# Two-layer block in fp32 on one core: the feed-forward down product in pairs of column chunks, three of eight steps with seven block products

## The chip, the cores and the metric

One core of a Trainium2 chip. The metric is device time in microseconds (us). A whole two-layer block for 256 tokens of width 2048 runs in one launch. TensorE multiplies, ScalarE (ACT) and VectorE (DVE) prepare operands and read results, SyncE (SP) issues the weight stream, GpSimd (POOL) a few other transfers.

## The reference

Everything is fp32. The part that matters here is the feed-forward of the second layer, with D = 2048 and D_FF = 8192:

```python
u = _rmsnorm(h, norm_mlp_g[layer])
a = jnp.einsum('bsd,df->bsf', u, w_up[layer])
a = jnp.square(jax.nn.relu(a))
h = h + jnp.einsum('bsf,fd->bsd', a, w_down[layer])
return _rmsnorm(h, norm_final_g)
```

## The kernel before, in words

**Exact products from three rounded ones.** Every fp32 operand is split into a rounded part (hi, type f32r) and the rest (lo). A product is three matmuls into the same bank: hi x hi, hi x lo, lo x hi. Activations are split once. Weights are split as they arrive.

**The stream.** All weights lie in one array of 359 units of 128 x 2048 fp32 (1 MB). SyncE loads unit u into slot u mod 4 of `raw`. Each unit is two pieces of 1024 columns. For piece n, ScalarE copies it into `w_hi` (L971, `split`), VectorE subtracts to get `w_lo` (L1404), TensorE uses both. The ring has RING = 4 piece slots: piece n+4 goes into the slot of piece n. `w_used` starts at 4 and TensorE raises it by one behind the last matmul of a piece; ScalarE waits for it, then raises `w_rounded`, VectorE waits for that and raises `w_rest`, which TensorE and SyncE wait for.

**The order of an engine's work.** It is written out by hand. `pieces(n, slot)` on ScalarE and VectorE goes through n pieces of the current product; for the j-th of them it splits the piece that lies four ahead and then calls `slot(j)`, other work put there. Each engine runs its own program strictly in order.

**The feed-forward.** w_up and w_down are cut into four slabs of 2048 hidden columns. A slab first makes the hidden activations in eight chunks of 256 columns (`project_up`, L887 and L890, banks of 512 with hidden columns as rows), four pieces each; VectorE squares them, ScalarE and VectorE split them into m_hi and m_lo. Then follow four down chunks of 512 output columns (`project`, L512 to L514), eight pieces each, for two tiles of 128 tokens. Of proj's four banks a chunk fills two, and the next chunk fills the other two while VectorE adds the finished ones, scaled, to `nat` (`add_scaled`, L1940). Four more banks (tbank, bank_a, bank_b) are idle in the feed-forward. Slabs 1 and 2 are one hardware loop on TensorE, ScalarE and VectorE. The last chunk of all is `project_last`: token tile 0 first, then tile 1, with four extra slots for weights.

**A border between chunks.** VectorE's reads of a finished chunk stand behind the last call of `pieces` for that chunk, and so behind the split of the fourth piece of the next one:

```python
dve.wait_ge(w_rounded, piece.at(1))
V.tensor_tensor(lo[:, s, :], raw[...], hi[:, s, :].bitcast(f32), SUB).then_inc(w_rest, 1)
...
pieces(slot=slot)
if not (end and d == 3):
    add_scaled(d)
```

Of the kernel before, what the change touches and what calls it, by code (L numbers as in the profile page):

```python
# [24 lines left out]
N_SLABS = 4  # L25
# [3 lines left out]
RING = 4  # L29
# [6 lines left out]
UNITS = 1 + 4 * (4 + 4 + 8 + 4 + 2 + 8) + 14 + 4 * (4 + 4 + 4) + 4 * 8 + 4 * 4 + 4 * N_SLABS * 8  # L36

# [76 lines left out]
def build(nc, stream, x_in, consts_in, early_in, params_in, pos_in, dft_in, alibi_in, fg_in, wf_in, z_store, ga_store, gb_store,  # L114
# [6 lines left out]
    with ctx:  # L121
# [59 lines left out]
        fg = place("fg", [P, D], f32, 144.25)  # L181

# [63 lines left out]
        inv3_sq = little("inv3_sq", [P, TT])  # L246
        inv4 = little("inv4", [P, TT])
# [9 lines left out]
        bank_b = psum("bank_b")  # L257
        x_banks = tbank + [proj[2], proj[3], bank_a, bank_b] + tbank
# [91 lines left out]
        tile_done = sem("tile_done")  # L350
        out_ready = sem("out_ready")
# [13 lines left out]

        PIECES = 2 * UNITS


        @block.sync
        def _(sp):  # L370
# [12 lines left out]
            whole, rest = divmod(UNITS - RING, RING)  # L383
# [90 lines left out]
        def _(pe):  # L474
# [423 lines left out]
            def hidden_before(j):  # L898
                pe.wait_ge(m_rest, up.at() - UP_CHUNKS + j + 1)

# [21 lines left out]
            def slab(head=None, before=None, end=False):  # L922
# [6 lines left out]
                if end:  # L929
                    project_last()  # L930
                else:
                    project(m_hi, m_lo)

            def up_head(j):
                if j == 1:
                    m_head(2)
                    m_head(3)

            def up_before(j):
                m_before(2 * j + 1)  # L940

            slab(up_head, up_before)
            with loop(pe, N_SLABS - 2, {piece: 64, chunk: UP_CHUNKS + 4, up: UP_CHUNKS}):
                slab()
            slab(end=True)
# [4 lines left out]
        def _(act):  # L950
            piece, done, chunk, tr, seq = Tally(), Tally(), Tally(), Tally(), Tally()
            sums = Tally()
# [8 lines left out]
            def split(n=1):  # L961
                for _ in range(n):
                    if piece.reg is None and piece.n >= PIECES:
                        return
                    u = piece.n // 2
                    if piece.n % 2 == 0:
# [1158 lines left out]
```

## Time and profile before

| | us |
|---|---|
| median of 3 runs (2145.39 to 2145.77) | 2145.61 |
| profiled execution | 2145.35 |
| its span | 2143.4 |
| TensorE busy | 2120.6 |
| VectorE busy | 1213.8 |
| ScalarE busy | 1022.7 |

The page shows TensorE at a granted clock of nine tenths or more in all 40 slices and busy nine tenths or more in all but the first and the last. Times are microseconds unless marked ns; L12 is line 12 of the kernel; a matmul's own duration (0.39 us for 128x512) overlaps that of its neighbours, so the distance from start to start is what it costs.

### The profile page before, as it was taken

To read this page: it belongs to the slowest core of one execution; us is meant where nothing else is said; L and a number is where in the kernel's file an instruction comes from. 1 tells how busy PE (TensorE), PEld (TensorE's weight loads), DVE (VectorE), ACT (ScalarE), POOL (GpSimd) and SP (SyncE) were. 2 spreads that over 40 slices of the span, in tenths; PEclk is the share of its full clock that TensorE was granted. 3 is DMA by queue.
4 is the path that set the end of the run, shared out by engine and by line. 5 is a ranking of instruction groups with operands and counts; after the bars stand their busy time and mean duration, and the time that the engine had idled before them with its cause. 6 is when DMAs were issued, how large, how long until landed. Compare 5 with 4: busy or idle time off the path is not lost.

```text
span 2143.4 us, 26531 instructions
## 1 busy us (share of the span) xinstructions
PE 2120.6 (99%) x10172; PEld 1772.7 (83%) x10172; DVE 1213.8 (57%) x1508; ACT 1022.7 (48%) x1301; POOL 37.8 (2%) x49
## 2 busy tenths in 40 slices
PE   8999999999999999999999999999999999999998
PEld 7888888888888877788888888888888888888886
DVE  5874545545555775556554454466556555655655
ACT  6444454445444674454454453454434434434443
POOL 0000000000000020000000000000000000000000
PEclk9999999999999999999999999999999999999999
DMA  7555555564565544365755542445555555555553
GB/s 268 177 196 190 189 192 193 196 235 177 177 218 194 190 145 157 121 233 196 291 185 187 179 157 96 177 176 199 195 196 188 186 196 192 183 194 196 183 192 117
DMA packets 56548, 402.44 MB, mean 188 GB/s; under 512 B 6240, under 2 KB 6496, under 8 KB 9216
## 3 DMA queue, kind: packets, MB, share of 16 engines
q1 hardware_dynamic: 53648, 380.67, 49.6%
q0 software_dynamic: 2656, 19.81, 2.4%
q8 instruction: 75, 1.23, 0.2%
q10 hardware_dynamic: 144, 0.52, 0.1%
q14 instruction: 25, 0.20, 0.0%
HBM read 392.59 MB, written 8.39 MB: 187 GB/s over the span
## 4 chain that ended last, share of the span: by engine, by line
PE 97%; ACT 1%; issue 1%; DVE 0%; DMA 0%; SPq 0%; POOLq 0%; POOL 0%; DVEq 0%; ACTq 0%
PE proj L512 25%; PE proj L514 24%; PE proj L513 24%; PE proj L887 11%; PE proj L890 6%; PE tbank L488 2%; PE bank_a L689 1%; ACT w_hi L971 1%; PE bank_a L686 0%; DMA nat<-x 0%; PE proj L817 0%; PE bank_b L843 0%; PE bank_a L831 0%; PE bank_a L767 0%; PE bank_b L783 0%
## 5 line engine op out<-in xcount | busy, mean ns | idle before, releaser
L1404 DVE TENSOR_TENSOR w_lo<-raw,w_hi 128x1024 fp32r<-128x1024 f32 x714 | 873.9, 1225 | 871.1 <-ACT w_hi L971 862.0
L971 ACT ACTIVATE w_hi<-raw 128x1024 fp32r<-128x1024 f32 x714 | 756.8, 1060 | 1043.9 <-PE proj L514 846.5
L512 PE MATMUL proj<-w_hi,a_both 128*128 128x512 f32 x1728 | 686.5, 397 | 0.0
L514 PE MATMUL proj<-w_hi,a_both 128*128 128x512 f32 x1728 | 674.1, 390 | 0.0
L513 PE MATMUL proj<-w_lo,a_both 128*128 128x512 f32 x1728 | 672.6, 389 | 0.0
L514 PEld LDWEIGHTS proj<-w_hi,a_both 128*128 128x128 f32 x1728 | 324.4, 188 | 69.2
L512 PEld LDWEIGHTS proj<-w_hi,a_both 128*128 128x128 f32 x1728 | 324.6, 188 | 68.4 <-issue 4.3
L513 PEld LDWEIGHTS proj<-w_lo,a_both 128*128 128x128 f32 x1728 | 324.9, 188 | 65.0
L887 PE MATMUL proj<-a_both,w_hi 128*128 128x512 f32 x1024 | 256.7, 392 | 0.3 <-DVE a_both L1432 0.3
L887 PEld LDWEIGHTS proj<-a_both,w_hi 128*128 128x128 f32 x1024 | 184.3, 189 | 34.1 <-DVE a_both L1432 0.5
L512 PE MATMUL proj<-w_hi,m_hi 128*128 128x512 f32 x480 | 186.8, 389 | 0.0
L513 PE MATMUL proj<-w_lo,m_hi 128*128 128x512 f32 x480 | 186.8, 389 | 0.0
L514 PE MATMUL proj<-w_hi,m_lo 128*128 128x512 f32 x480 | 186.7, 389 | 0.0
L890 PEld LDWEIGHTS proj<-a_both,w_lo 128*128 128x128 f32 x1024 | 139.7, 190 | 10.0
L890 PE MATMUL proj<-a_both,w_lo 128*128 128x256 f32 x1024 | 142.8, 282 | 0.0
L514 PEld LDWEIGHTS proj<-w_hi,m_lo 128*128 128x128 f32 x480 | 90.1, 188 | 18.8
L512 PEld LDWEIGHTS proj<-w_hi,m_hi 128*128 128x128 f32 x480 | 90.1, 188 | 18.5
L513 PEld LDWEIGHTS proj<-w_lo,m_hi 128*128 128x128 f32 x480 | 90.1, 188 | 18.5
L512 PE MATMUL proj<-w_hi,lat_hi 128*128 128x512 f32 x112 | 45.6, 407 | 0.3 <-DVE v_b L1801 0.3
L514 PE MATMUL proj<-w_hi,lat_lo 128*128 128x512 f32 x112 | 43.9, 392 | 0.0
L513 PE MATMUL proj<-w_lo,lat_hi 128*128 128x512 f32 x112 | 43.7, 390 | 0.0
L1432 DVE SCALAR_TENSOR_TENSOR a_both<-tbank,par,a_both 128x256 fp32r<-128x256 f32 x56 | 24.1, 476 | 9.9 <-ACT a_both L1004 9.8
(298 smaller groups left out, 1169.1 us busy)
## 6 DMA issues: line engine op xcount, KB each, us to landing
raw<-stream SPq DMA_DIRECT2D x359, 1024.0 KB, 4.8
nat<-x SPq DMA_DIRECT2D x4, 512.0 KB, 8.3
z_store<-z POOLq DMA_DIRECT2D x1, 2048.0 KB, 8.2
ga_store<-z POOLq DMA_DIRECT2D x1, 2048.0 KB, 12.4
gb_store<-z POOLq DMA_DIRECT2D x4, 512.0 KB, 7.9
yb<-z_store POOLq DMA_DIRECT2D x4, 512.0 KB, 7.9
ga<-ga_store POOLq DMA_DIRECT2D x1, 2048.0 KB, 8.1
gb<-gb_store POOLq DMA_DIRECT2D x1, 2048.0 KB, 14.3
```

The costliest lines, as they stand in the source:

```text
L488: last = nc.tensor.transpose(tbank[tr.n % 2][:, b * P:(b + 1) * P], src(b), ident)
L512: nc.tensor.matmul(banks[t][:, :], ah, wh, start=first, stop=False)
L513: nc.tensor.matmul(banks[t][:, :], ah, wl, start=False, stop=False)
L514: last = nc.tensor.matmul(banks[t][:, :], al, wh, start=False, stop=end)
L689: last = nc.tensor.matmul(bank_a[:, to:to + keys], qr_t[r, h // 2, t * P:(t + 1) * P], kr_t[r, h // 2, 0:keys], start=False, stop=(t == TT ...
L887: nc.tensor.matmul(banks[f], w_hi[:, s, cols], a_both[:, kt, :, :].rearrange("p s t -> p (s t)"), start=(kt == 0), stop=False)
L890: last = nc.tensor.matmul(banks[f][:, 0:TOK], w_lo[:, s, cols], a_hi[:, kt, :], start=False, stop=(kt == KT - 1))
L971: A((w_hi_end if extra else w_hi)[:, piece.n % RING, :], raw[:, u % RING, (piece.n % 2) * PIECE:(piece.n % 2 + 1) * PIECE], ACT.Copy).then ...
L1404: V.tensor_tensor(lo[:, s, :], raw[:, u % RING, (piece.n % 2) * PIECE:(piece.n % 2 + 1) * PIECE], hi[:, s, :].bitcast(f32), SUB).then_inc( ...
L1432: last = V.scalar_tensor_tensor(lo[:, kt + f, :], b[:, f * TOK:(f + 1) * TOK], par_c(g, i + f), hi[:, kt + f, :].bitcast(f32), MUL, SUB)
```

## The change

The four down chunks of a slab become two pairs of column chunks; seven pairs in all, numbered q = 0 to 6, since the last slab keeps its last two chunks in the old form. A pair is eight steps over the hidden dimension (256 rows each), and a step has all four outputs at once: two token tiles by two column blocks of 512. Its unit of weights has four blocks of 512: two of hidden rows by two of columns. Five steps (0, 2, 4, 6, 7) do the plain eight block products of three matmuls. Steps 1, 3 and 5 do Winograd's form of Strassen's 2x2 product: VectorE adds up four combinations of the weight blocks (`sum_weights`) and four of the activation blocks (`sum_hidden`), and seven block products follow. Four of them go to banks of their own (`mixed`), three into the banks of the plain outputs (`whole`), and VectorE puts mixed ones together into the outputs (`add_mixed`). So a pair uses all eight banks; the next pair swaps the two sets of four.

A summed step's unit takes four ring pieces instead of two (1024, 512, 1024 and 1024 columns, the last two from `w_sum`), a pair 22 pieces. Step 7 (`end_step`) takes the four outputs one after another, tile 1 first, and signals each (`part_done`), but frees its two pieces together at its end. `part_read` counts VectorE's reads, five a pair: one in part 2 of `add_mixed`, four in `add_whole`. The slab loops are written out. The core of the diff (left out: declarations, ScalarE's form of the split, which follows the same table of pieces, the host's order of the blocks in a unit, the unchanged split of the piece table, the two chunks at the end, which keep their matmuls):

```diff
+STEPS = 8
+SUM_AT = (1, 3, 5)
+PAIRS = 2 * N_SLABS - 1
+END_ORDER = (2, 3, 0, 1)
...
+        if u in SUM_UNITS:
+            where += [(u, 0, PIECE, False), (u, PIECE, CW, False), (u, 0, PIECE, True), (u, PIECE, PIECE, True)]
+        else:
+            where += [(u, 0, PIECE, False), (u, PIECE, PIECE, False)]
...
+            def product(bank, hi, lo, wh, wl, first=False, end=False):
+                nc.tensor.matmul(bank[:, :], hi, wh, start=first, stop=False)
+                nc.tensor.matmul(bank[:, :], hi, wl, start=False, stop=False)
+                return nc.tensor.matmul(bank[:, :], lo, wh, start=False, stop=end)
...
+            def plain_step(step, whole):
+                for h in range(2):
+                    pe.wait_ge(w_rest, piece.at(1))
+                    for t in range(TT):
+                        tok = slice(t * P, (t + 1) * P)
+                        for n in range(2):
+                            last = product(whole[2 * t + n], m_hi[:, 2 * step + h, tok], m_lo[:, 2 * step + h, tok],
+                                           *weights(0, n), first=(step == 0 and h == 0))
+                    last.then_inc(w_used, 1)
+                    piece.add()
+            def sum_step(step, whole, mixed):
+                i = SUM_AT.index(step)
+                t0, t1 = slice(0, P), slice(P, TOK)
+                a, b = 2 * step, 2 * step + 1
+                first, end = i == 0, i == len(SUM_AT) - 1
+                pe.wait_ge(w_rest, piece.at(1))
+                product(mixed[0], m_hi[:, a, t0], m_lo[:, a, t0], *weights(0, 0), first=first, end=end)
+                product(whole[0], m_hi[:, b, t0], m_lo[:, b, t0], *weights(0, 1)).then_inc(w_used, 1)
+                piece.add()
+                pe.wait_ge(ms_rest, sums.at(i + 1))
+                pe.wait_ge(w_rest, piece.at(1))
+                product(whole[1], ms_hi[:, i, 3, :], ms_lo[:, i, 3, :], *weights(0, 0)).then_inc(w_used, 1)
+                piece.add()
+                pe.wait_ge(w_rest, piece.at(1))
+                product(mixed[1], ms_hi[:, i, 1, :], ms_lo[:, i, 1, :], *weights(0, 0), first=first, end=end)
+                product(mixed[3], ms_hi[:, i, 0, :], ms_lo[:, i, 0, :], *weights(0, 1), first=first,
+                        end=end).then_inc(w_used, 1)
+                piece.add()
+                pe.wait_ge(w_rest, piece.at(1))
+                product(mixed[2], ms_hi[:, i, 2, :], ms_lo[:, i, 2, :], *weights(0, 0), first=first, end=end)
+                product(whole[2], m_hi[:, b, t1], m_lo[:, b, t1], *weights(0, 1)).then_inc(w_used, 1)
+                piece.add()
+            def end_step(step, whole):
+                pe.wait_ge(w_rest, piece.at(2))
+                for o in END_ORDER:
+                    tok = slice(o // 2 * P, (o // 2 + 1) * P)
+                    for h in range(2):
+                        last = product(whole[o], m_hi[:, 2 * step + h, tok], m_lo[:, 2 * step + h, tok],
+                                       *weights(h, o % 2), end=(h == 1))
+                    if o != END_ORDER[-1]:
+                        last.then_inc(part_done, 1)
+                last.then_inc(w_used, 2)
+                piece.add(2)
+            def pair(q):
+                whole, mixed = parts[q % 2], parts[1 - q % 2]
+                if q:
+                    pe.wait_ge(part_read, 5 * (q - 1) + 1)
+                else:
+                    pe.wait_ge(t_by_dve, by_dve.at())
+                for step in range(STEPS):
+                    if q % 2 == 0:
+                        pe.wait_ge(m_rest, up.at() - UP_CHUNKS + step + 1)
+                    if step == SUM_AT[0]:
+                        if q % 2 == 0:
+                            pe.wait_ge(proj_read, chunk.at() * 2)
+                        else:
+                            pe.wait_ge(part_read, 5 * q)
+                    if step in SUM_AT:
+                        sum_step(step, whole, mixed)
+                    elif step == STEPS - 1:
+                        end_step(step, whole)
+                    else:
+                        plain_step(step, whole)
...
+            for n in range(N_SLABS):
                 for c in range(UP_CHUNKS):
                     up.add()
-                    project_up(slot=head if c == 0 else None, before=before if c == 0 else None)
-                project(m_hi, m_lo, before=hidden_before)
-                for j in range(2):
+                    if n and c < 2:
+                        pe.wait_ge(part_read, 5 * (2 * n - 1) + (3, 5)[c])
+                    assert chunk.n % 2 == 1 - c % 2
+                    first = n == 0 and c == 0
+                    project_up(slot=(lambda j: (m_head(2), m_head(3)) if j == 1 else None) if first else None,
+                               before=(lambda j: m_before(2 * j + 1)) if first else None)
+                pair(2 * n)
+                if n < N_SLABS - 1:
+                    pair(2 * n + 1)
+                else:
+                    pe.wait_ge(part_read, 5 * (PAIRS - 1) + 1)
                     project(m_hi, m_lo)
...
+            def round_sums(i):
+                act.wait_ge(ms_summed, ms_sums.at(i + 1))
+                A(ms_hi[:, i, :, :], ms[:, :, :], ACT.Copy).then_inc(ms_rounded, 1)
...
+            def pair(q):
+                for step in range(STEPS):
+                    def slot(j):
+                        if q % 2 == 0 and step == 0 and j == 0:
+                            round_hidden(UP_CHUNKS - 1)
+                        if step == SUM_AT[-1] + 1 and j == 0:
+                            act.wait_ge(w_used, done.at(RING))
+                            if q % 2:
+                                act.wait_ge(part_read, 5 * (q - 1) + 1)
+                            else:
+                                act.wait_ge(proj_read, chunk.at() * 2)
+                            A(stg[:, 0, :], parts[1 - q % 2][0][:, :], ACT.Copy).then_inc(m_copied, 1)
+                    pieces(4 if step in SUM_AT else 2, slot=slot)
...
+                    u, at, width, summed = WHERE[piece.n]
+                    s = piece.n % RING
+                    if u in SUM_UNITS and piece.n == FIRST_PIECE[u]:
+                        sum_weights(u)
+                    src = raw[:, u % RING, at:at + width]
+                    if summed:
+                        src = w_sum[:, (w_sums.n - 1) % 2, at:at + width]
                     dve.wait_ge(w_rounded, piece.at(1))
-                    u, s = piece.n // 2, piece.n % RING
                     extra = piece.reg is None and piece.n >= PIECES - RING
                     hi, lo = (w_hi_end, w_lo_end) if extra else (w_hi, w_lo)
-                    V.tensor_tensor(lo[:, s, :], raw[:, u % RING, (piece.n % 2) * PIECE:(piece.n % 2 + 1) * PIECE],
-                                    hi[:, s, :].bitcast(f32), SUB).then_inc(w_rest, 1)
+                    V.tensor_tensor(lo[:, s, 0:width], src, hi[:, s, 0:width].bitcast(f32), SUB).then_inc(w_rest, 1)
                     piece.add()
+            def sum_weights(u):
+                dve.wait_ge(raw_landed[u % RING], (u // RING + 1) * 16)
+                b = raw[:, u % RING, :].rearrange("p (b c) -> p b c", b=4)
+                s = w_sum[:, w_sums.n % 2, :].rearrange("p (b c) -> p b c", b=4)
+                w_sums.add()
+                wait(dve, w_rest, piece.n - 4)
+                V.tensor_tensor(s[:, 0:2, :], b[:, 0:3:2, :], b[:, 3, :].unsqueeze(1).to_broadcast([P, 2, CW]),
+                                ADD).then_inc(w_summed, 1)
+                dve.wait_ge(w_summed, w_sums.at() * 2 - 1)
+                chain(V.tensor_tensor(s[:, 2, :], s[:, 0, :], b[:, 2, :], ADD))
+                V.tensor_tensor(s[:, 3, :], s[:, 2, :], b[:, 1, :], ADD).then_inc(w_summed, 1)
...
+            def sum_hidden(c):
+                dve.wait_ge(up_squared, up.at(c + 1))
+                wait(dve, ms_rest, ms_sums.at(SUM_AT.index(c)))
+                m = stg2[:, c % 2, :].rearrange("p (b c) -> p b c", b=4)
+                V.tensor_tensor(ms[:, 0, :], m[:, 0, :], m[:, 1, :], ADD)
+                chain(V.tensor_tensor(ms[:, 1, :], m[:, 1, :], m[:, 3, :], SUB))
+                chain(V.tensor_tensor(ms[:, 2, :], m[:, 3, :], ms[:, 0, :], SUB))
+                V.tensor_tensor(ms[:, 3, :], m[:, 2, :], ms[:, 2, :], ADD).then_inc(ms_summed, 1)
+            def rest_of_sums(i):
+                dve.wait_ge(ms_rounded, ms_sums.at(i + 1))
+                V.tensor_tensor(ms_lo[:, i, :, :], ms[:, :, :], ms_hi[:, i, :, :].bitcast(f32), SUB).then_inc(ms_rest, 1)
+            def add_mixed(q, part):
+                mixed, n1 = parts[1 - q % 2], 2 * (q % 2)
+                out = lambda t, n: nat[:, t, (n1 + n) * CW:(n1 + n + 1) * CW]
+                u, w = stg[:, 0, :], stg[:, 1, :]
+                if part == 0:
+                    dve.wait_ge(w_used, done.at(RING))
+                    wait(dve, part_read, 5 * q)
+                    dve.wait_ge(m_copied, q + 1)
+                    V.scalar_tensor_tensor(out(0, 0), u, inv3_sq[:, 0:1], out(0, 0), MUL, ADD).then_inc(dve_seq, 1)
+                    seq.add()
+                    chain(V.tensor_tensor(u, mixed[2][:, :], u, ADD))
+                    chain(V.tensor_tensor(w, mixed[1][:, :], u, ADD))
+                if part == 1:
+                    chain(V.tensor_tensor(u, mixed[3][:, :], u, ADD))
+                    V.scalar_tensor_tensor(out(0, 1), w, inv3_neg[:, 0:1], out(0, 1), MUL, ADD).then_inc(dve_seq, 1)
+                    seq.add()
+                    chain(V.scalar_tensor_tensor(out(1, 0), u, inv3_neg[:, 1:2], out(1, 0), MUL, ADD))
+                if part == 2:
+                    V.tensor_tensor(w, mixed[1][:, :], u, ADD).then_inc(part_read, 1)
+                    dve.wait_ge(part_read, 5 * q + 1)
+                    V.scalar_tensor_tensor(out(1, 1), w, inv3_sq[:, 1:2], out(1, 1), MUL, ADD).then_inc(dve_seq, 1)
+                    seq.add()
+            def add_whole(q):
+                whole, n1 = parts[q % 2], 2 * (q % 2)
+                dve.wait_ge(dve_seq, seq.at())
+                for i, o in enumerate(END_ORDER):
+                    t, n = o // 2, o % 2
+                    if i < 3:
+                        dve.wait_ge(part_done, 3 * q + i + 1)
+                    else:
+                        dve.wait_ge(w_used, done.at(RING))
+                    y = nat[:, t, (n1 + n) * CW:(n1 + n + 1) * CW]
+                    V.scalar_tensor_tensor(y, whole[o][:, :], inv3_sq[:, t:t + 1], y, MUL, ADD).then_inc(part_read, 1)
+            def pair(q):
+                for step in range(STEPS):
+                    def slot(j):
+                        if q % 2 == 0 and step == 0 and j == 1:
+                            rest_of_hidden(UP_CHUNKS - 1)
+                        if step == SUM_AT[-1] + 1:
+                            add_mixed(q, j)
+                        if step == SUM_AT[-1] + 2 and j == 0:
+                            add_mixed(q, 2)
+                    pieces(4 if step in SUM_AT else 2, slot=slot)
+                add_whole(q)
...
```

On ScalarE and VectorE the slab is now: eight up chunks with `sum_hidden`, `round_sums` and `rest_of_sums` in their slots, then `pair(2 * n)` and, but in the last slab, `pair(2 * n + 1)`.

## Rows read from the trace of the kernel before

**Rows 1.** The page: span, and busy us, share and instructions by engine.
```profile
span 2143.4 us, 26531 instructions
PE 2120.6 (99%) x10172; PEld 1772.7 (83%) x10172; DVE 1213.8 (57%) x1508; ACT 1022.7 (48%) x1301; POOL 37.8 (2%) x49
```
**Rows 2.** The page: the chain that ended last, by engine.
```profile
PE 97%; ACT 1%; issue 1%; DVE 0%; DMA 0%; SPq 0%; POOLq 0%; POOL 0%; DVEq 0%; ACTq 0%
```
**Rows 3.** Stretches: an up and a down product (PE, PEld, DVE, ACT, POOL; PEclk, DMA, GB/s).
```profile
1605.56:1694.75 89.19, 89.19 (x512) 78.49 (x512) 53.55 (x55) 40.99 (x46) 0.00 (x0) 1.00 0.54 189
1694.75:1782.00 87.25, 87.23 (x387) 71.93 (x385) 45.68 (x42) 34.96 (x34) 0.00 (x0) 1.00 0.55 193
```
**Rows 4.** Timeline at a chunk's end: start, duration, operation, count, idle before and releaser.
```profile
1779.30 1.06 ACT L971 ACTIVATE w_hi<-raw 128x1024 fp32r<-128x1024 f32 x1 [1.66 <-PE proj L514]
...
1781.37 0.39 PE L513 MATMUL proj<-w_lo,m_hi 128*128 128x512 f32 x1
...
1781.59 0.39 PE L514 MATMUL proj<-w_hi,m_lo 128*128 128x512 f32 x1
...
1782.00 2.10 PE L887 MATMUL proj<-a_both,w_hi 128*128 128x512 f32 x8
1782.02 1.06 ACT L971 ACTIVATE w_hi<-raw 128x1024 fp32r<-128x1024 f32 x1 [1.66 <-PE proj L514]
1783.11 1.23 DVE L1404 TENSOR_TENSOR w_lo<-raw,w_hi 128x1024 fp32r<-128x1024 f32 x1 [1.49 <-ACT w_hi L971]
...
1784.25 1.64 DVE L1940 SCALAR_TENSOR_TENSOR nat<-proj,inv_sq,nat 128x512 f32<-128x512 f32 x2
```
**Rows 5.** Groups of instructions, 1500 to 2143 us: busy, mean ns, idle before.
```profile
L1404 DVE TENSOR_TENSOR w_lo<-raw,w_hi 128x1024 fp32r<-128x1024 f32 x224 | 274.5, 1226 | 266.5 <-ACT w_hi L971 263.7 <-DVE nat L1940 2.1
L971 ACT ACTIVATE w_hi<-raw 128x1024 fp32r<-128x1024 f32 x224 | 237.8, 1061 | 349.7 <-PE proj L514 192.4 <-PE proj L890 157.3
...
L1940 DVE SCALAR_TENSOR_TENSOR nat<-proj,inv_sq,nat 128x512 f32<-128x512 f32 x30 | 22.4, 747 | 2.2 <-DVE nat L1940 0.8
L1932 DVE TENSOR_TENSOR m_lo<-stg,m_hi 128x512 fp32r<-128x512 f32 x27 | 18.5, 684 | 0.0
...
L1338 ACT ACTIVATE m_hi<-stg 128x512 fp32r<-128x512 f32 x27 | 16.5, 612 | 0.0
...
L1977 DVE TENSOR_TENSOR nat<-nat,fg 128x1024 f32<-128x1024 f32 x3 | 3.6, 1216 | 0.0
```
**Rows 6.** Timeline: two VectorE operations, the second waiting for the first.
```profile
1442.55 0.68 DVE L1962 TENSOR_TENSOR stg<-proj,stg 128x512 f32<-128x512 f32 x1
...
1443.27 0.69 DVE L1966 SCALAR_TENSOR_TENSOR stg<-stg 128x512 f32<-128x512 f32 x1
```
**Rows 7.** The page: issues of the weight stream, KB each, us to landing.
```profile
raw<-stream SPq DMA_DIRECT2D x359, 1024.0 KB, 4.8
```
**Rows 8.** Timeline: TensorE released by VectorE after a short wait.
```profile
1435.49 1.65 DVE L1432 SCALAR_TENSOR_TENSOR a_both<-tbank,par,a_both 128x256 fp32r<-128x256 f32 x4
...
1437.20 2.14 PE L887 MATMUL proj<-a_both,w_hi 128*128 128x512 f32 x8 [0.31 <-DVE a_both L1432]
```
**Rows 9.** The end: TensorE's last matmul, then two stretches with the granted clock.
```profile
2134.96 0.39 PE L918 MATMUL proj<-w_hi_end,m_lo 128*128 128x512 f32 x1
...
2136.50:2137.00 0.50, 0.00 (x0) 0.00 (x0) 0.08 (x1) 0.39 (x2) 0.00 (x0) 1.00 0.00 0
2137.00:2137.50 0.50, 0.00 (x0) 0.00 (x0) 0.23 (x2) 0.00 (x0) 0.15 (x1) 0.85 0.00 0
```
**Rows 10.** Timeline of TensorE at the start.
```profile
12.29 1.11 PE L555 MATMUL bank_a<-cst,nat 128*128 128x128 f32 x4 [1.64 <-DMA nat<-x]
...
14.05 1.91 PE L555 MATMUL tbank<-cst,nat 128*128 128x128 f32 x8
...
17.26 0.41 PE L572 MATMUL proj<-a_both,w_hi 128*128 128x256 f32 x1
17.47 0.38 PE L573 MATMUL proj<-a_both,w_lo 128*128 128x256 f32 x1
...
18.63 0.28 PE L573 MATMUL proj<-a_both,w_lo 128*128 128x256 f32 x1
18.75 0.28 PE L571 MATMUL proj<-a_both,w_hi 128*128 128x256 f32 x1
```

More of the change, by code:

```diff
@@ L257, in build @@
         bank_b = psum("bank_b")
+        parts = (tbank + [bank_a, bank_b], proj)
         x_banks = tbank + [proj[2], proj[3], bank_a, bank_b] + tbank
@@ L920, in project_last, with weights @@
                 chunk.add()
-            def slab(head=None, before=None, end=False):
+            def product(bank, hi, lo, wh, wl, first=False, end=False):
+                nc.tensor.matmul(bank[:, :], hi, wh, start=first, stop=False)
+                nc.tensor.matmul(bank[:, :], hi, wl, start=False, stop=False)
+                return nc.tensor.matmul(bank[:, :], lo, wh, start=False, stop=end)
+            def weights(ahead, half, k=0):
+                s = (piece.n + ahead) % RING
+                cols = slice(half * CW, (half + 1) * CW)
+                return w_hi[:, s, cols], w_lo[:, s, cols]
@@ L928, in slab @@
                     project(m_hi, m_lo)
-                if end:
                     project_last()
[L931 to L944, printed above, removed]
@@ L945, in _ @@
-            slab(end=True)
+                sums.add(len(SUM_AT))
             assert piece.n == PIECES, (piece.n, PIECES)
@@ L1356, in slab, with slot @@
                     chunk.add()
-                for d in range(4):
-                    def slot(j, d=d):
-                        if d == 0 and j == 1:
-                            round_hidden(UP_CHUNKS - 1)
-                        if end and d and j == 3:
-                            res_squares(d - 1, 16 + 8 * (N_SLABS - 1) + 2 * d)
-                    pieces(slot=slot)
-                    chunk.add()
-                up.add(UP_CHUNKS)
-            up = Tally()
-            slab(first=True)
-            with loop(act, N_SLABS - 2, {piece: 64, done: 64, chunk: UP_CHUNKS + 4, up: UP_CHUNKS}):
-                slab()
-            slab(end=True)
+                pair(2 * n)
+                if n < N_SLABS - 1:
+                    pair(2 * n + 1)
+                up.add(UP_CHUNKS)
+                ms_sums.add(len(SUM_AT))
+            def slot(j):
+                if j in (3, 5):
+                    act.wait_ge(part_read, 5 * PAIRS)
+                    chunk_squares((j - 3) // 2)
+            pieces(slot=slot)
+            chunk.add()
+            pieces(slot=lambda j: res_squares(2, 18) if j == 3 else None)
+            chunk.add()
             for t in range(TT):
-                act.wait_ge(res_ready, 16 + 8 * N_SLABS - 1 + t)
+                act.wait_ge(res_ready, 19 + t)
                 square_sum(stg2[:, t, :], nat[:, t, 3 * CW:4 * CW], ss2[:, t, 3:4])
@@ L1386, in _ @@
         def _(dve):
-            piece, done, chunk, tr, seq, his = (Tally() for _ in range(6))
+            piece, done, chunk, tr, seq, his, w_sums = (Tally() for _ in range(7))
             V = nc.vector
@@ L1966, in slab @@
                     V.scalar_tensor_tensor(s, s, 0.0, s, MAX, MUL).then_inc(up_squared, 1)
[L1967 to L1988 removed]
+                pair(2 * n)
+                if n < N_SLABS - 1:
+                    pair(2 * n + 1)
+                up.add(UP_CHUNKS)
+                ms_sums.add(len(SUM_AT))
+            pieces(slot=lambda j: weigh((j - 4) // 2) if j in (4, 6) else None)
+            add_scaled(2)
+            pieces(slot=lambda j: weigh(2) if j == 4 else None)
             def last_chunk(t):
@@ L2021, in _units_up, with _pair_units @@
     return v.reshape(-1, P, 4 * CW)
+def _pair_units(w):
+    v = w.reshape(STEPS, 2, P, 2, 2, CW)
+    r = np.empty((2, STEPS, P, 4, CW), w.dtype)
+    for step in range(STEPS):
+        order = ((0, 0), (1, 0), (1, 1), (0, 1)) if step in SUM_AT else ((0, 0), (0, 1), (1, 0), (1, 1))
+        for b, (k, n) in enumerate(order):
+            r[:, step, :, b, :] = v[step, k, :, :, n, :].transpose(1, 0, 2)
+    return r.reshape(-1, P, 4 * CW)
 def _stream(i):
```

111 lines of the change are left out of this document (70 added, 41 removed).

## The prediction

> **What bounds the kernel now.** First the page's busy times: TensorE is busy 99% of the span, VectorE and ScalarE about half [rows 1]. Then the chain that ended last: 97% of it is TensorE [rows 2]. So a matmul saved is its time saved, provided TensorE never waits. Then the stretches of one slab: the up product fills 89.19 of 89.19 us, the down product 87.23 of 87.25 us, with VectorE busy 53.55 and 45.68 us [rows 3]. The timeline of a chunk border gives the beat: consecutive 128x512 matmuls start 0.22 to 0.23 us apart, and ScalarE starts rounding one weight piece 2.72 us after another (1779.30, 1782.02), twelve matmuls, 0.2267 us each [rows 4]. A down step of two pieces (24 matmuls) is 5.44 us. This is the arithmetic to keep for everything below.
>
> The same rows show what the prediction turns on: how far VectorE runs ahead. Both splitting engines stay four pieces ahead, and piece n+4 goes into the slot that piece n frees. Let T be the moment when the next matmul would start if nothing waited (1781.59 + 0.23 = 1781.82). The last piece of the chunk frees its slot, ScalarE starts at T+0.20 (1782.02), VectorE's subtraction at T+1.29 (1783.11), and only then, at T+2.43 (1784.25), comes VectorE's first read of the finished banks, because in VectorE's program it stands behind that subtraction. Today this is free: the next chunk writes the other two of proj's four banks [rows 4].
>
> **What is removed.** Three steps in each of seven pairs need 7 block products of three matmuls instead of 8: 7 x 3 x 3 = 63 matmuls, 63 x 0.2267 = 14.3 us, on the path. Nothing else leaves TensorE. The slab loops are unrolled; a loop's return cost 1782.00 - 1781.82 = 0.2 us [rows 4], which I count as nothing, the more so since unrolled code must be fetched.
>
> **What VectorE gets inside a pair.** Single operations, 128x1024 subtraction 1.226, 128x512 0.684, with a bank as input and a scale 0.747, a broadcast input 1.216 us [rows 5]. An operation that waits for the one before starts 0.72 us after it (1442.55, 1443.27) [rows 6]; one that doesn't starts 1.14 us after a 1.23 us subtraction (1783.11, 1784.25) [rows 4], 0.09 earlier. A summed step: three additions of weights 1.26 + 0.72 + 0.60 = 2.6 (the 1024-wide one first, by the broadcast row; the trace has no addition of this very kind, so its ends are the 0.68 of a 512-wide and twice that), subtractions 1.14 + 0.60 + 1.14 + 1.14 = 4.0, together 6.6 us beside 21 x 0.2267 = 4.76 us of TensorE. A plain step: 2.3 beside 5.44. Mixed outputs 5.6 (eight operations), whole outputs 2.8, late hidden rest 0.6. Sum of a pair: 3 x 6.6 + 5 x 2.3 + 5.6 + 2.8 + 0.6 = 40.3 us beside 3 x 4.76 + 5 x 5.44 = 41.5 us. That is 97% full, so I followed it piece by piece: a step that begins at 0 with piece 0. In the first pair of a slab piece 6 is ready at 9.7 and wanted at 10.2, piece 8 at 14.6 against 15.6, piece 14 at 24.4 against 25.8. The four-piece ring carries each surplus of 1.9 us into the plain step behind it. Inside a pair I count no stall; if each summed step ran 0.5 us over, that would be 21 x 0.5 = 10 us. ScalarE has 3 x 1.06 + 0.6 = 3.8 us in a summed step, under 4.76, and costs nothing [rows 5]. In the up product the sums of activations (four small operations and a 0.68, under 3 us for a chunk of 11.2 us) fit in 89.19 - 53.55 = 35.6 us of free VectorE time [rows 3]. The stream moves the same bytes; a unit lands 4.8 us after its issue and is asked for four units ahead [rows 7], so I leave it at nothing; the weight additions also need it at most one step earlier than the rounding does.
>
> **What the pair's borders get.** Now there are eight outputs in eight banks, and the next product needs banks that VectorE has still to read. The last read of the mixed outputs (add_mixed part 2) stands in step 7 behind the split of piece 24 of the pair (22 pieces, so the third of the next phase). That piece goes into the slot of piece 20, the first of step 7, and end_step frees both its pieces only after its last matmul. So whatever the early signals part_done say, VectorE is stuck on w_rounded, which is stuck on w_used, until T. Parts 0 and 1 are done before: step 6's first piece ends at T-8.16, its successor is rounded by T-6.9, three operations and the next subtraction run to T-2.45, three more to T-0.3.
>
> (a) From the first pair of a slab to the second, three times: VectorE first sums the weights of the next pair's step 1 (T-0.3 to T+2.3), subtracts piece 24 (to T+3.45) and makes the last read (0.72, T+4.2). TensorE restarted 0.06 us after such a release (1435.49 + 1.65 = 1437.14, 1437.20) [rows 8]. Stall 4.2 us, 12.6 in all.
> (b) From pair 6 to the plain chunk 2: no sum of weights, so subtraction from T+1.3, read from T+2.45, stall 3.2 us.
> (c) From a second pair to the next up product, three times: TensorE asks for three reads, the mixed one and two whole ones. Read T+2.45 to 3.17, its scaled add to 3.85, split of the 25th piece to 5.0, two scaled adds with a bank (0.67 and 0.75) to T+6.4. Stall 6.5 us, 19.5 in all.
>
> The second waits (a pair's step 1, the second up chunk) come 5.4 and 11.2 us later, when the four whole outputs are read (T+4.2 to T+9 against T+9.6 in (a)): nothing, with 0.5 us to spare. Stalls together 12.6 + 3.2 + 19.5 = 35.3 us. The bounds: if additions of weights cost half, (a) is 3.2 (-3 us); if VectorE enters the border 1.5 us late, (a) grows by that and (b) and (c) don't (+4.5).
>
> **The clock.** TensorE has no idle gap as long as these in the body of this trace. At the end, its last matmul ends at 2134.96 + 0.39 = 2135.35 and the granted clock, 1.00 until 2137.0, reads 0.85 in the half microsecond behind: it fell to half (1.2 of 2.4 GHz) at about 2137.35, 2.0 us after the last work [rows 9]. Every stall above is longer. At the start, 128x256 matmuls came 0.21 us apart (17.26, 17.47) and 0.12 apart later (18.63, 18.75); the engine had then worked without a gap since 14.05, and nearly since 12.29 [rows 10]. The change of beat falls at 17.68, so a return at half rate lasts 3.6 to 5.4 us and costs half of that, 1.8 to 2.7 us. I take 2.0 us and five of the seven stalls, all three of 6.5 us and two of the others: 10 us. Ends: none, 0; all seven at 2.7, 19 us. The Trainium skill, "TensorE: Matmul & The Clock Gate" (Part 1), has half rate as the default that only sustained activity lifts, and its section "HAM oscillation" charges half of all throttled time. The trace agrees in both halves; no row of it shows a gap in the middle of work.
>
> **Sum.** The profiled execution took 2145.35 us (span 2143.4), 0.26 below the median shown. 2145.35 - 14.3 + 35.3 + 10 = 2176.4; plus 0.26, 2176.6 us. Behind the last matmul nothing changes: chunks 2 and 3 of the last slab keep their form, and the squares and gains of the first two columns move into chunk 2, where each engine is half idle.
>
> **Rivals.**
> 1. The stalls come, the clock holds: 2145.6 - 14.3 + 35.3 = 2166.6. For it: the fall at the end follows a gap that never ended. Against: 2.0 us were enough. The skill's page would side with the forecast for the longest gaps.
> 2. VectorE is late inside the pairs as well. For it: 40.3 of 41.5 us, and a margin of 0.5 us at piece 6. Ten more microseconds at 0.5 us a summed step, and (a) grows by 4.5: 2176.6 + 15 = 2191.
> 3. The other side: VectorE reaches the reads before TensorE needs the banks. It decides whether the split in step 7 waits for that step's end. Were piece 24's slot free at the middle of end_step (T-2.7), the last mixed read would end at T+0.5 to T+1.5 and the first whole reads at T+3.8, and with one piece less in front before T: the 63 matmuls would be the result, 2145.6 - 14.3 = 2131.3. Against: two w_used increments come together on the last matmul, and today's reads come at T+2.43 in every chunk.
> 4. The sums don't shorten the product. 7 products of 3 matmuls in the diff leave no room; a change of the beat could. Without the 14.3 us: 2190.9.
>
> **How the numbers follow.** Forecast 0.60; rival 1 0.17; rival 2 0.12; rival 4 0.03; rival 3 0.04; a half way to it that ends near no change 0.04. The range 2158 to 2192 us goes 8 us under rival 1 (stalls of some 27 instead of 35 us) and up to rival 2; that leaves out 2 in 10. What a measurement of this kernel can tell from no change is about 0.2%, 4.3 us. Faster 0.05, same 0.02, slower 0.93.
>
> **What would show it.** In the profile after: 63 matmuls fewer; idle before seven groups of matmuls, released by VectorE, of 4.2 (three), 3.2 (one) and 6.5 us (three); a granted clock under 1.00 in about five short stretches behind them, with 128x512 matmuls 0.43 us apart; the last mixed read in each pair behind a weight subtraction, 2.4 to 3.5 us after end_step's last matmul; VectorE over 90% busy in the pairs and no TensorE gap inside them. It is wrong if the borders show gaps under 1 us, if the gaps lie inside summed steps, or if matmuls keep their 0.2267 us right behind a 6.5 us gap.

## The result and the profile after

The changed kernel takes 2179.71 us (median of 5 runs, 2178.94 to 2182.61) against 2145.53 us: ratio 1.0161, 95% interval 1.0147 to 1.0175. It is 34.2 us slower with 63 matmuls fewer. The forecast was 2176.6. The five runs differ more than those of the kernel before, and the slowest has the lowest mean granted clock (0.989, the others 0.991 and 0.992).

The page of the kernel after: span, busy times by engine, the chain by engine. They answer to [rows 1, 2].

```profile
span 2176.9 us, 25919 instructions
PE 2119.2 (97%) x10109; PEld 1768.6 (81%) x10109; DVE 1352.8 (62%) x1730; ACT 1064.7 (49%) x1362; POOL 37.8 (2%) x49
...
PE 94%; DVE 2%; ACT 2%; issue 1%; DMA 0%; SPq 0%; POOLq 0%; POOL 0%; DVEq 0%; ACTq 0%
```

TensorE has 10109 matmuls instead of 10172 and yet nearly the same busy time, and the chain now gives 2% each to VectorE and ScalarE (before, 0% and 1%). Who TensorE waited for from 1500 us on (total us, times, longest), the same kernel:

```profile
PE proj L929 <- DVE nat L2150: 19.4, 3, 6.7
PE proj L963 <- DVE stg L2134: 12.2, 3, 4.1
PE proj L554 <- DVE stg L2134: 3.1, 1, 3.1
```

These are all of its waits there: three before the up products, three at pairs 1, 3 and 5, one before chunk 2. The same list of the kernel before is empty. The timeline of the border from pair 0 to pair 1 (start, duration, operation), with T = 1559.61 + 0.23 = 1559.84:

```profile
1559.59 1.23 DVE L1566 TENSOR_TENSOR w_sum<-raw 128x1024 f32<-128x1024 f32 x1
1559.61 0.39 PE L965 MATMUL tbank<-w_hi,m_lo 128*128 128x512 f32 x1
1560.10 1.58 ACT L1092 ACTIVATE w_hi<-raw 128x1024 fp32r<-128x1024 f32 x2 [4.44 <-PE tbank L965]
1560.85 0.69 DVE L1569 TENSOR_TENSOR w_sum<-w_sum,raw 128x512 f32<-128x512 f32 x1
1561.58 0.69 DVE L1570 TENSOR_TENSOR w_sum<-w_sum,raw 128x512 f32<-128x512 f32 x1
1562.18 1.22 DVE L1556 TENSOR_TENSOR w_lo<-raw,w_hi 128x1024 fp32r<-128x1024 f32 x1
1563.32 0.68 DVE L2134 TENSOR_TENSOR stg<-proj,stg 128x512 f32<-128x512 f32 x1
...
1564.06 0.80 PE L963 MATMUL proj<-w_hi,m_hi 128*128 128x512 f32 x1 [4.06 <-DVE stg L2134]
...
1565.51 0.63 PE L963 MATMUL proj<-w_hi,m_hi 128*128 128x512 f32 x1
1565.93 0.63 PE L964 MATMUL proj<-w_lo,m_hi 128*128 128x512 f32 x1
```

These lines show the whole mechanism: VectorE sums weights from T-0.25, subtracts piece 24 at T+2.34 and makes the last mixed read at T+3.48; TensorE goes on at T+4.22, and then its matmuls start 0.43 us apart, not 0.23. The border from pair 1 to the up product, T = 1608.49:

```profile
1608.26 0.39 PE L965 MATMUL proj<-w_hi,m_lo 128*128 128x512 f32 x1
1608.74 2.00 ACT L1092 ACTIVATE w_hi<-raw 128x1024 fp32r<-128x1024 f32 x2 [4.44 <-PE proj L965]
1609.90 1.23 DVE L1556 TENSOR_TENSOR w_lo<-raw,w_hi 128x1024 fp32r<-128x1024 f32 x1 [1.70 <-ACT w_hi L1092]
1611.05 0.68 DVE L2134 TENSOR_TENSOR stg<-tbank,stg 128x512 f32<-128x512 f32 x1
1611.77 0.75 DVE L2136 SCALAR_TENSOR_TENSOR nat<-stg,inv_sq,nat 128x512 f32<-128x512 f32 x1
1612.43 1.22 DVE L1556 TENSOR_TENSOR w_lo<-raw,w_hi 128x1024 fp32r<-128x1024 f32 x1
1613.57 2.72 DVE L2150 SCALAR_TENSOR_TENSOR nat<-proj,inv_sq,nat 128x512 f32<-128x512 f32 x4
1615.03 3.41 PE L929 MATMUL proj<-a_both,w_hi 128*128 128x512 f32 x8 [6.38 <-DVE nat L2150]
```

Here the mixed read comes at T+2.56 (today's +2.43 [rows 4]), and TensorE goes on at T+6.54. Stretches of the same kernel (length; busy PE, PEld, DVE, ACT, POOL; granted clock; DMA; GB/s):

```profile
1518.33:1559.84 41.51, 41.51 (x185) 34.18 (x183) 35.38 (x39) 22.15 (x24) 0.00 (x0) 1.00 0.53 195
1559.84:1562.90 3.06, 0.16 (x1) 0.00 (x0) 2.99 (x4) 1.58 (x2) 0.00 (x0) 1.00 0.60 252
1562.90:1569.70 6.80, 5.64 (x13) 4.47 (x14) 5.09 (x8) 0.06 (x1) 0.00 (x0) 0.53 0.46 154
1569.70:1575.00 5.30, 5.30 (x24) 4.33 (x23) 2.43 (x2) 3.00 (x3) 0.00 (x0) 0.96 0.01 3
2122.00:2126.00 4.00, 1.16 (x5) 0.98 (x6) 3.00 (x4) 1.81 (x2) 0.00 (x0) 1.00 0.34 141
```

Inside pair 0 (the first line) TensorE never waits; its 183 matmuls take 41.51 us, 0.2268 each. At this border the clock falls to half while TensorE is still idle, about 1563, and is back at about 1570. The last line is the restart before chunk 2, where it does not fall.

### The profile page after: what moved, and what is told of

The parts are those of the page before. It is cut to its first block, busy times and chain, and to the rows that moved or that the text cites. A ratio compares the mean times of both kernels' runs of the same rounds, so it can differ in the third digit from the quotient of the medians.

```text
span 2176.9 us, 25919 instructions
## 1 busy us (share of the span) xinstructions
PE 2119.2 (97%) x10109; PEld 1768.6 (81%) x10109; DVE 1352.8 (62%) x1730; ACT 1064.7 (49%) x1362; POOL 37.8 (2%) x49
## 4 chain that ended last, share of the span: by engine, by line
PE 94%; DVE 2%; ACT 2%; issue 1%; DMA 0%; SPq 0%; POOLq 0%; POOL 0%; DVEq 0%; ACTq 0%
PE proj L554 20%; PE proj L556 19%; PE proj L555 19%; PE proj L929 11%; PE proj L932 6%; PE proj L963 2%; PE proj L964 2%; PE proj L965 2%; PE tbank L530 2%; PE tbank L963 1%; PE tbank L964 1%; PE tbank L965 1%; ACT w_hi L1092 1%; DVE w_lo L1556 1%; PE bank_a L731 1%
## 5 line engine op out<-in xcount | busy, mean ns | idle before, releaser
L1556 DVE TENSOR_TENSOR w_lo<-raw,w_hi 128x1024 fp32r<-128x1024 f32 x714 | 858.2, 1209 | 731.8 <-ACT w_hi L1092 722.8
L1092 ACT ACTIVATE w_hi<-raw 128x1024 fp32r<-128x1024 f32 x714 | 744.6, 1047 | 943.8 <-PE proj L556 667.4
L929 PE MATMUL proj<-a_both,w_hi 128*128 128x512 f32 x1024 | 261.5, 398 | 19.7 <-DVE nat L2150 19.4
L1092 ACT ACTIVATE w_hi<-w_sum 128x1024 fp32r<-128x1024 f32 x42 | 44.6, 1061 | 91.8 <-PE proj L965 37.2
L963 PE MATMUL proj<-w_hi,m_hi 128*128 128x512 f32 x150 | 61.2, 408 | 12.2 <-DVE stg L2134 12.2
L1556 DVE TENSOR_TENSOR w_lo<-w_sum,w_hi 128x1024 fp32r<-128x1024 f32 x42 | 51.4, 1223 | 33.3 <-ACT w_hi L1092 33.3
L964 PE MATMUL proj<-w_lo,m_hi 128*128 128x512 f32 x150 | 60.7, 405 | 0.0
L965 PE MATMUL proj<-w_hi,m_lo 128*128 128x512 f32 x150 | 60.4, 403 | 0.0
L963 PEld LDWEIGHTS proj<-w_hi,m_hi 128*128 128x128 f32 x150 | 29.6, 197 | 19.7 <-DVE stg L2134 13.4
L963 PE MATMUL tbank<-w_hi,m_hi 128*128 128x512 f32 x101 | 39.3, 390 | 0.0
## 6 DMA issues: line engine op xcount, KB each, us to landing
ga_store<-z POOLq DMA_DIRECT2D x1, 2048.0 KB, 12.5
```

Source lines behind the costliest of these rows:

```text
L929: nc.tensor.matmul(banks[f], w_hi[:, s, cols], a_both[:, kt, :, :].rearrange("p s t -> p (s t)"), start=(kt == 0), stop=False)
L963: nc.tensor.matmul(bank[:, :], hi, wh, start=first, stop=False)
L964: nc.tensor.matmul(bank[:, :], hi, wl, start=False, stop=False)
L965: return nc.tensor.matmul(bank[:, :], lo, wh, start=False, stop=end)
L1092: A((w_hi_end if extra else w_hi)[:, piece.n % RING, 0:width], src, ACT.Copy).then_inc(w_rounded, 1)
L1556: V.tensor_tensor(lo[:, s, 0:width], src, hi[:, s, 0:width].bitcast(f32), SUB).then_inc(w_rest, 1)
```

## The experiments

All are timed in 3 rounds against the kernel before (2145.33 us beside e1 to e4, 2145.47 us beside e5 to e7).

**e1: the last mixed read one split earlier.**

```diff
-                        if step == SUM_AT[-1] + 2 and j == 0:
+                        if step == SUM_AT[-1] + 1 and j == 1:
                             add_mixed(q, 2)
```

> The changed kernel with the last mixed read (part 2 of add_mixed) in step 6 behind part 1, in front of the split of piece 24 instead of behind it. Nothing else moves. Theory (order in VectorE's program): the read ends at T+0.4, so the first matmuls of pairs 1, 3, 5 and of chunk 2 wait 0.4 to 0.5 us instead of 4.2 and 3.4. But VectorE then has the weight sums, two splits and four whole reads behind it, to T+8.2, and the next pair's step 1 wants them at T+5.9: 2.3 us of new stall there, three times. Before the up products: split to T+2.45, split to 3.6, two whole reads to 5.0, stall 5.0 instead of 6.5. Sum 3 x 2.8 + 0.5 + 3 x 5.0 = 23.9 instead of 36 us, and the clock falls three times, not six (7 us instead of 11): 2163. Rival (the banks themselves are late, or TensorE's own results are what VectorE waits for): the gaps at pairs 1, 3, 5 stay near 4 us, 2180. Rival (late operands within the pairs matter): gain under 5 us, since VectorE's work is the same.

Measured: 2166.74 us (2164.27 to 2168.1). TensorE's waits from 1500 us on:

```profile
PE proj L929 <- DVE nat L2150: 15.0, 3, 5.2
PE tbank L963 <- DVE nat L2150: 6.0, 3, 2.0
PE proj L963 <- DVE stg L2134: 1.0, 3, 0.3
PE proj L554 <- DVE stg L2134: 0.3, 1, 0.3
```

Four waits were named beforehand as 5.0, 2.3, 0.45 and 0.45 us; they are 5.0, 2.0, 0.3 and 0.3 on average. So it is the order in VectorE's program, and a part of a removed wait comes back at the next reader of the same queue. The clock was a miss: three falls were expected, the profiled execution has six. Each of the three 2.0 us waits at step 1 brings one too, 0.1 to 0.8 us after work has begun again. The first of them:

```profile
1568.02 0.50 PE L963 MATMUL tbank<-w_hi,m_hi 128*128 128x512 f32 x1 [2.00 <-DVE nat L2150]
...
1567.00:1569.50 2.50, 1.48 (x5) 1.26 (x6) 2.50 (x4) 0.18 (x1) 0.00 (x0) 0.87 0.94 390
1569.50:1570.50 1.00, 1.00 (x4) 0.71 (x4) 0.73 (x1) 0.14 (x1) 0.00 (x0) 0.50 0.11 25
```

Over the 8 us behind each of these three restarts the granted clock is 0.79, so a fall costs 8 x 0.21 = 1.7 us and the three 5.0 us. The profiled execution, the slowest of the four with 2168.1 us, lies 5.1 us over the 2163 expected.

**e2: step 7 frees its two pieces one after the other.** (The two loops of end_step change places.)

```diff
-                for o in END_ORDER:
+                for h in range(2):
+                    pe.wait_ge(w_rest, piece.at(1))
+                    for o in END_ORDER:
...
-                last.then_inc(w_used, 2)
-                piece.add(2)
+                    last.then_inc(w_used, 1)
+                    piece.add()
```

> The changed kernel with step 7's matmuls in the order of its two weight pieces (first piece for all four outputs, then the second), each piece freed at its own end, the outputs signalled in the last quarter. Theory: piece 24 can be rounded 2.72 us sooner. At a pair followed by a pair that buys nothing, VectorE is then summing weights until T+2.3 anyway: 4.1 us stays, three times. Before chunk 2: subtraction from T-0.3 to T+0.9, read T+1.6, stall 1.6 instead of 3.4. Before the up products: read T+1.6, scaled add 2.25, split 3.4, two whole reads 4.8, stall 4.9 instead of 6.6. Gain 1.8 + 3 x 1.7 = 7 us, clock nearly the same: 2172 to 2173. Rival (the freeing of both pieces at the end is the whole cause of the border gaps): all seven shrink by 2.7 us, 2161 or less. Rival (VectorE's queue has nothing to do with the ring): 2180.

Measured: 2170.65 us (2169.25 to 2171.33), 9.1 us under the changed kernel. The waits:

```profile
PE proj L929 <- DVE nat L2150: 14.1, 3, 4.7
PE proj L963 <- DVE stg L2134: 12.2, 3, 4.1
PE proj L554 <- DVE stg L2134: 1.5, 1, 1.5
```

Unchanged at 3 x 4.1 us where weight sums stand in front, 1.5 and 4.7 at the others, as worked out (1.6 and 4.9). The late freeing of the pieces is a cause at four borders of seven, and at those it explains a quarter to a half of the gap (1.8 of 6.5 us, 1.6 of 3.1). The waits shrink by 6.9 us in all; the other 2 us of the gain fit the clock, though this was not tested by itself: counted as in the table at e3, from the 8 us behind the six restarts, the falls cost 10.6 us here and 12.3 us in the changed kernel.

**e3: the waits filled with matmuls.**

```diff
+FILL = (15, 25, 15, 25, 15, 25, 10)
...
+                if FILL[q]:
+                    pe.wait_ge(m_copied, q + 1)
+                for i in range(FILL[q]):
+                    nc.tensor.matmul(mixed[0][:, :], m_hi[:, 15, 0:P], ..., start=True, stop=True)
```

> The changed kernel with extra matmuls (15, 25 and 10 of 128x512 behind pairs with a second pair, an up product and chunk 2 next) into the mixed bank that ScalarE has copied, overwritten by the next phase; the output is untouched. They last 3.4, 5.7 and 2.3 us, less than the waits they lie in, so the waits end when they did, and TensorE has under 1 us of idle. Theory (the clock costs 11 us of the 34): granted clock 1.00 all through, matmuls 0.227 apart behind every border, and 2179.7 - 11 = 2168 to 2169. Rival (matmuls behind a border are slow because VectorE reads banks or SBUF beside them): the 0.43 us spacing stays, 2180. Rival (extra matmuls are not hidden): 75 + 75... in all 130 matmuls x 0.227 = 30 us more, 2209.

Measured: 2167.94 us (2167.76 to 2168.1), though it does 130 matmuls more. Its waits, then TensorE behind the first border:

```profile
PE proj L930 <- DVE nat L2156: 2.4, 3, 1.0
PE proj L964 <- DVE stg L2140: 2.0, 3, 0.7
PE proj L555 <- DVE stg L2140: 0.9, 1, 0.9
```

```profile
1560.04 3.56 PE L1047 MATMUL proj<-m_hi 128*128 128x512 f32 x15
1564.26 0.50 PE L964 MATMUL proj<-w_hi,m_hi 128*128 128x512 f32 x1 [0.66 <-DVE stg L2140]
1564.59 0.40 PE L965 MATMUL proj<-w_lo,m_hi 128*128 128x512 f32 x1
1564.83 0.39 PE L966 MATMUL proj<-w_hi,m_lo 128*128 128x512 f32 x1
```

In this run pair 0 starts and ends 0.20 us later (T = 1560.04), so TensorE goes on at T+4.22, exactly as late as without the filling; the other six borders agree to 0.01 us as well. But its matmuls start 0.33 us, then 0.24 us apart, and the mean granted clock of the run is 0.999 for 0.991. VectorE reads the same banks beside the same matmuls, so neither banks nor ports made them slow. By the medians the half rate costs 2179.71 - 2167.94 = 11.8 us, by the two profiled executions 11.1. The lengths of the stretches behind the six falls, from TensorE's restart to the end of the pair or of the up product, give the cost of each (us; granted clock of the changed kernel in the 8 us behind the restart):

| behind the restart of | changed kernel | e3 | cost of the fall | clock |
|---|---|---|---|---|
| pair 1, 1564.06 | 44.43 | 41.61 | 2.8 | 0.62 |
| up product, 1615.03 | 90.80 | 89.49 | 1.3 | 0.82 |
| pair 3, 1751.55 | 42.97 | 41.62 | 1.4 | 0.82 |
| up product, 1801.35 | 91.41 | 89.50 | 1.9 | 0.73 |
| pair 5, 1938.49 | 43.20 | 41.65 | 1.6 | 0.79 |
| up product, 1988.23 | 91.81 | 89.50 | 2.3 | 0.68 |

Their sum is 11.3 us. In e3 the granted clock is 1.00 in all six stretches.

**e4: every read out from behind the split of step 7.** The core of the edit on VectorE:

```diff
-                        if step == SUM_AT[-1] + 1:
-                            add_mixed(q, j)
-                        if step == SUM_AT[-1] + 2 and j == 0:
-                            add_mixed(q, 2)
+                        if step == SUM_AT[-1] and j == 3:
+                            add_mixed(q, 0)
+                        if step == SUM_AT[-1] + 1 and j == 0:
+                            add_mixed(q, 1)
+                            if q % 2:
+                                add_whole(q, 0)
+                                add_whole(q, 1)
+                        if step == SUM_AT[-1] + 1 and j == 1:
...
+                            add_mixed(q, 2)
+                            for i in range(2 if q % 2 else 0, 3):
+                                add_whole(q, i)
+                        if step == STEPS - 1 and j == 0:
+                            add_whole(q, 3)
```

> The changed kernel with VectorE's reads out from behind the split of step 7: parts 0, 1, 2 of add_mixed behind the fourth piece of step 5 and the two pieces of step 6, whole outputs read as end_step signals them (three before the split of piece 24, two of them before part 2 where an up product follows), the fourth behind it; the next pair's step 1 asks for three reads, its third piece for the fourth. Same operations, same matmuls. Theory: part 2 ends at T-0.6 (T+0.1 with an up product next, where it isn't waited for), the whole reads that the up product wants at T-1.7, weight sums T+4.0, piece 24 at T+5.2 against T+5.4 wanted. Every border gap under 0.5 us, the clock stays at 1.00, and the 63 matmuls are all that is left: 2145.5 - 14.3 = 2131, at most 2134. Rival (VectorE at 97% of a pair is itself the bound): the gaps move from the borders into steps 1 and 3, a loss of 1 to 3 us a pair: 2140 to 2150. Rival (summed steps give less than 63 matmuls of time): 2146.

Measured: 2132.81 us (2132.64 to 2132.96), ratio to the kernel before 0.9942, interval 0.9925 to 0.9958. It beats both kernels. No matmul from 1500 us on waits for VectorE or ScalarE by TensorE's list. What is left are six short waits of its weight loads, at the start of step 1 and at its third piece in pairs 1, 3 and 5. The first list is the wait, the second the timeline at the start of step 1 in pair 1, the third pair 1 and pair 6:

```profile
PEld tbank L963 <- issue: 2.7, 6, 0.5
```

```profile
1563.99 1.22 DVE L1557 TENSOR_TENSOR w_lo<-raw,w_hi 128x1024 fp32r<-128x1024 f32 x1
1564.95 0.39 PE L965 MATMUL proj<-w_hi,m_lo 128*128 128x512 f32 x1
1565.36 0.47 PE L963 MATMUL tbank<-w_hi,m_hi 128*128 128x512 f32 x1
1565.67 0.39 PE L964 MATMUL tbank<-w_lo,m_hi 128*128 128x512 f32 x1
```

```profile
1559.73:1601.87 42.14, 42.03 (x184) 34.20 (x183) 39.53 (x44) 22.09 (x23) 0.00 (x0) 1.00 0.53 197
2037.23:2078.74 41.51, 41.51 (x185) 34.35 (x184) 36.78 (x41) 22.14 (x24) 0.00 (x0) 1.00 0.53 192
```

Two waits make pair 1 0.6 us longer than pair 6: 0.26 us at the start of step 1, where VectorE's subtraction ends only at 1563.99 + 1.22 = 1565.21, and 0.34 us at the third piece. Expected was that piece at T+5.2, and it is ready at T+5.5 (T = 1559.73). Three times 0.6 is 1.8 us, and 2145.33 - 14.3 + 1.8 = 2132.8. VectorE is busy 39.53 of 42.14 us in pair 1.

**e5: e4 with the eighth product back.**

```diff
-                product(mixed[0], ..., first=first, end=end)
+                product(mixed[0], ..., first=first, end=False)
+                product(mixed[0], ..., first=False, end=end)
```

> e4 with eight block products in each summed step again: the first one (three matmuls into mixed[0]) is issued twice, so the outputs hold it twice. 63 matmuls more, nothing else. Theory (a matmul on the path is worth its beat, and nothing else of the gain comes from elsewhere): 2132.8 + 63 x 0.2267 = 2147.1, less up to 1.5 us where the longer step 1 covers e4's six small waits of 0.25 us: 2145.6 to 2147.1. Rival (VectorE, not TensorE, sets the pace in the pairs): under half of it comes back, below 2140.

Measured: 2146.57 us (2145.85 to 2146.97), 13.8 us over e4. Three of the six small waits are gone, those at the third piece, covered by the longer step (3 x 0.34 = 1.0 us):

```profile
PEld tbank L963 <- issue: 1.2, 3, 0.4
```

Pair 6, which has no wait in either run, gives the price of a matmul directly. In e5 it takes 43.55 us, nine matmuls more than in e4:

```profile
2049.08:2092.63 43.55, 43.55 (x194) 36.05 (x193) 36.88 (x41) 22.15 (x24) 0.00 (x0) 1.00 0.52 183
```

43.55 - 41.51 = 2.04 us, 0.227 each, or 14.3 us for 63. (By the medians it would be 13.8 + 1.0 = 14.8; in the profiled executions 0.76 us of that lies ahead of pair 0, which starts at 1518.98 in e5 and at 1518.22 in e4.) Against the kernel before, e5 is a tie, ratio 1.0004, interval 0.9995 to 1.0014: with as many matmuls as before, the sums and the use of all eight banks cost nothing that the time shows, once the reads stand right.

**e6 and e7: more VectorE work in each summed step of e4**, 0.72 and 1.26 us: one addition of `sum_weights` is done twice, in e6 the last, in e7 the first.

```diff
+                chain(V.tensor_tensor(s[:, 3, :], s[:, 2, :], b[:, 1, :], ADD))
                 V.tensor_tensor(s[:, 3, :], s[:, 2, :], b[:, 1, :], ADD).then_inc(w_summed, 1)
```

```diff
+                chain(V.tensor_tensor(s[:, 0:2, :], b[:, 0:3:2, :], b[:, 3, :].unsqueeze(1).to_broadcast([P, 2, CW]),
+                                      ADD))
                 V.tensor_tensor(s[:, 0:2, :], b[:, 0:3:2, :], b[:, 3, :].unsqueeze(1).to_broadcast([P, 2, CW]),
                                 ADD).then_inc(w_summed, 1)
```

> e4 with the last 512-wide weight addition done twice in each of the 21 summed steps, 0.72 us of VectorE each. Theory (the pair is 97% full, but the ring and the waits on ScalarE absorb a small surplus; only a pair right behind another has none left, where e4 waits 0.25 us twice): 0.7 to 1.0 us in three pairs, 2135 to 2136. Rival (VectorE is the bound through the pair): 21 x 0.72 = 15 us, 2148. Rival (VectorE has real room): 2132.8.

> e4 with the 1024-wide weight addition done twice in each of the 21 summed steps, 1.26 us of VectorE each; a pair then has 42.6 + 1.5 us of VectorE beside 41.5 us of TensorE. Theory: worked piece by piece, 1.5 to 2.5 us in each of the three pairs right behind another and about 0.3 us in each of the four others: 2132.8 + 4.5 + 1.2 to + 7.5 + 1.2, 2138 to 2142. Rival (bound through the pair): 26.5 us, 2159. Rival (room): under 2134.

Measured: e6 2135.51 us (2135.1 to 2135.72), 2.7 over e4, e7 2140.01 us (2139.66 to 2140.46), 7.2 over. TensorE's waits in e6, then in e7:

```profile
PE tbank L963 <- DVE w_lo L1557: 2.2, 3, 0.8
```

```profile
PE tbank L963 <- DVE w_lo L1557: 3.9, 3, 1.3
PE proj L963 <- DVE w_lo L1557: 0.9, 4, 0.2
```

21 additions of 0.72 us, 15 us of VectorE time, cost 2.7, and 26 us cost 7.2. The first waits lie only in the three pairs right behind a pair; with 1.26 us the four others begin to wait, 0.2 us each by this list, which leaves out the waits of the weight loads: pair 6, which has no pair in front, takes 42.12 us in e7 for 41.51 in e4, 0.6 us more where 0.3 was expected. So the pair was nearly full and not over full, as the piece-by-piece working had it.

## Why the prediction was right

**The saved matmuls**: 14.3 forecast; pair 6 of e5 beside that of e4 gives 0.227 us each, 14.3 in all. Rival 4, that the sums don't shorten the product, is out.

**The border stalls**: 3 x 4.2 + 3.2 + 3 x 6.5 = 35.3 forecast. Measured, idle plus the 0.16 us by which a matmul's own duration outlasts its beat: 12.2 + 3.1 + 19.4 + 7 x 0.16 = 35.8 us. The stations of the way agree to 0.15 us (weight sums at T-0.25 for T-0.3, restart at T+4.22 for T+4.2, T+6.54 for T+6.5; chunk 2 waited 3.3 for 3.2), but for the second of the three up products, which starts at T+6.83. The second waits, with 0.5 us to spare by the forecast, did not occur, not even in e3 at full clock. The reason is shown and not only argued: moving one read by one split (e1), freeing a slot sooner (e2) and moving all reads (e4) each moved the gaps by what the working gave. The guess for an addition of two raw blocks, 1.26 us, was right: 1.22 and 0.04 of wait.

**Inside the pair**: no stall forecast, none seen. Rival 2 is out. Its price, 10 us for 0.5 us a summed step, was too high as well, as far as e4 can stand for the changed kernel: there 0.72 us more a summed step cost 2.7 us and not 21 x 0.72, so most of it was absorbed; that the ring and VectorE's waits for ScalarE do this is argued, not shown by itself. One sign was put wrongly: VectorE over 90% busy inside the pairs. In pair 0 of the changed kernel it is 85% (35.38 of 41.51), because 4.1 us of its work for the pair lie in the stall behind it; together that is 39.5 us beside the 40.3 added up. Only in e4, where the work lies inside, is a pair behind a pair at 94%.

**The clock**: this term was right by its sum more than by its parts. Forecast were five falls of seven at 2.0 us, 10 us. Six occur, one at every border of 4.1 us or more and none at chunk 2's 3.1 us, and they cost 11.3 us, 1.9 each. The cold start, the only row at hand for the length of a return, gave the right mean and neither the spread of 1.3 to 2.8 us nor its cause: what a fall costs depends on how much of the half rate lies in the wait and how much in the work behind it. At the up product of 1615.03 the clock fell in the middle of the wait, and 8 matmuls took 3.24 us, 1.4 us over their 1.81; at 1564.06 it fell about 0.8 us before the restart, and 14 matmuls (3.2 us) took 6.1 us. That the mean came out so near is in part luck. The rule of the Trainium skill, "TensorE: Matmul & The Clock Gate" (HAM oscillation), that a long wait for data brings half rate and that throttled time counts half, is now borne out in the middle of a kernel: counted by half, the granted clocks of the table give 12.3 us, the lengths 11.3. Rival 1 (2166.6) is what e3 looks like: 2167.94.

**The sum**, for the profiled execution: 2145.35 - 14.3 + 35.8 + 11.3 = 2178.2, measured 2178.94.

**Rival 3**, the faster side, tied its 2131.3 to the wrong condition, a slot freed in the middle of step 7. e2 frees it there and takes 2170.65 us: VectorE's weight sums still stand in front of the read at three borders, and whole reads at three others. The text of the rival says as much, with reads at T+0.5 to T+1.5 and T+3.8 that leave stalls, and so 2131.3 did not follow from it. The time itself can be had by another way, the place of the reads: e4 runs 2132.8. The forecast and all four rivals took the order of the reads as given.

## What to carry to other kernels

When a product takes all accumulation banks, ask for each read of a finished bank what stands in front of it in the reading engine's program, and whether that can finish before the producer does; a prefetch that waits for the producer's own last step turns a free read into a stall. Price a border stall with the half clock behind it: here a third on top, and it varies from run to run. A saving of matmuls is worth its beat only when the borders are clean: the same 63 matmuls gave +34 us or -12.5 us by the place of eight reads.

## What the runs showed of the hardware

In e1 a wait of 2.0 us, begun some 5.7 us after the end of one of 0.3 us, was enough for a fall to half rate, three times of three, the first 0.8 us after work had begun again. In the changed kernel a lone wait of 3.1 us before chunk 2 was not (granted clock 1.00 there, 2122 to 2126 us). So the length of a wait alone did not decide it in these runs; what else does is not shown. Matmuls whose results nobody reads, issued into a bank already read, held the full rate over waits of 3 to 6.5 us and made the kernel 11.8 us faster (e3).
